# Third and fourth weight sums of a Strassen-like product started later in a pair, on GpSimd

## The reference

```
D_FF = 3 * D_MODEL; FFN_CONV = 3
h = rms_norm(x, g_ffn_pre)
up = h @ w_up                                  # (1024 x 1024) @ (1024 x 6144)
gate_h = causal_dwconv(up[..., :D_FF], ffn_conv_w, ffn_conv_b)
hid = gelu(gate_h) * up[..., D_FF:]
x = x + rms_norm(hid @ w_down, g_ffn_post)
```

## Time and profile before

| | us |
|---|---|
| median of 3 runs (lowest, highest) | 3272.5 (3272.47, 3274.01) |
| the profiled execution's own time | 3272.96 |
| its span in the trace | 3271.2 |
| PE busy | 3088.3 (94%) |
| DVE busy | 2314.0 (71%) |
| ACT busy | 1473.5 (45%) |
| POOL busy | 981.6 (30%) |

### The profile page before, as it was taken

One profiled execution on the slowest core, in us unless ns is written; L12 is line 12 of the kernel. 1 busy time (PEld: TensorE's weight loads), 2 busy tenths in 40 slices (PEclk: granted clock), 3 DMA queues, 4 the chain that ended last, 5 costly groups with the idle time before them and its releaser, 6 DMA issues.

```text
span 3271.2 us, 44920 instructions
## 1 busy us (share of the span) xinstructions
PE 3088.3 (94%) x14885; PEld 2455.6 (75%) x14885; DVE 2314.0 (71%) x2995; ACT 1473.5 (45%) x2003; POOL 981.6 (30%) x511
## 2 busy tenths in 40 slices
PE   6999998888998799999969999999989999999998
PEld 5668776566786688888857888888767777778867
DVE  7788967886545899999966775633588888811266
ACT  4345433667222788888841366201443343300142
POOL 2224342000341011111104433345234444434432
PEclk8999999999998899999989999999999999999999
DMA  7223221340242999999972222134133333454312
GB/s 263 71 63 93 65 65 52 110 120 30 81 160 85 378 382 379 380 382 382 352 267 60 64 83 87 41 120 145 64 91 104 114 103 108 155 206 148 115 33 71
DMA packets 365271, 496.54 MB, mean 152 GB/s; under 512 B 34478, under 2 KB 237148, under 8 KB 365156
## 3 DMA queue, kind: packets, MB, share of 16 engines
q1 hardware_dynamic: 350356, 460.39, 41.0%
q10 hardware_dynamic: 5440, 17.86, 1.7%
q0 software_dynamic: 9360, 16.80, 1.4%
HBM read 422.57 MB, written 83.92 MB: 155 GB/s over the span
## 4 chain that ended last, share of the span: by engine, by line
PE 43%; DVE 13%; issue 4%; SPq 3%; DMA 2%; ACT 2%; DVEq 0%; POOL 0%; ACTq 0%; POOLq 0%
PE acc L450 9%; PE acc L451 9%; PE acc L452 9%; PE acc L2049 3%; PE acc L2051 3%; PE acc L2050 3%; DVE TT L3064 3%; PE acc L2068 1%; PE acc L2070 1%; PE acc L2069 1%; DVE UWL L2817 1%; SPq L1952 1%; DVE uu L3070 1%; DVE TT L3073 1%; DMA mraw<-in_exp_w 1%
## 5 line engine op out<-in xcount | busy, mean ns | idle before, releaser
L421 POOL TENSOR_TENSOR whi<-wraw,one 128x1024 fp32r<-128x1024 f32 (+1 forms) x153 | 289.9, 1895 | 1312.2 <-PE acc L452 1014.4
L450 PE MATMUL acc<-Ah,whi 128*128 128x512 f32 (+1 forms) x1568 | 620.3, 396 | 4.6 <-POOL wlo L423 3.2
L452 PE MATMUL acc<-Ah,wlo 128*128 128x512 f32 (+1 forms) x1568 | 611.0, 390 | 0.0
L451 PE MATMUL acc<-Al,whi 128*128 128x512 f32 (+1 forms) x1568 | 611.0, 390 | 0.0
L423 POOL TENSOR_TENSOR wlo<-wraw,whi 128x1024 fp32r<-128x1024 f32 (+1 forms) x153 | 381.5, 2493 | 12.0
L450 PEld LDWEIGHTS acc<-Ah,whi 128*128 128x128 f32 (+1 forms) x1568 | 294.2, 188 | 81.5 <-issue 18.9
L451 PEld LDWEIGHTS acc<-Al,whi 128*128 128x128 f32 (+1 forms) x1568 | 294.4, 188 | 63.6 <-issue 3.1
L452 PEld LDWEIGHTS acc<-Ah,wlo 128*128 128x128 f32 (+1 forms) x1568 | 294.2, 188 | 62.6
L2162 DVE TENSOR_TENSOR mlo<-mraw,mhi 128x1024 fp32r<-128x1024 f32 x256 | 306.9, 1222 | 37.5 <-ACT mhi L2106 23.8
L2106 ACT ACTIVATE mhi<-mraw 128x1024 fp32r<-128x1024 f32 x256 | 267.8, 1063 | 74.5 <-PE acc L2051 51.6
L2049 PE MATMUL acc<-mhi,XTh 128*128 128x512 f32 x512 | 203.8, 398 | 3.6 <-DVE XTl L2157 3.3
(11 more groups left out here) (726 smaller groups left out, 6651.0 us busy)
## 6 DMA issues: line engine op xcount, KB each, us to landing
mraw<-in_exp_w SPq DMA_DIRECT2D x512, 256.0 KB
mraw<-in_exp_w SPq DMA_DIRECT2D x128, 512.0 KB, 12.1
wraw<-in_w_in SPq DMA_DIRECT2D x72, 512.0 KB, 3.8
TT<-in_ada_w SPq DMA_DIRECT2D x32, 512.0 KB, 3.8
TT<-gates SPq DMA_DIRECT2D x32, 512.0 KB, 4.6
wraw<-in_w_up SPq DMA_DIRECT2D x24, 512.0 KB, 4.7
hidTh<-hidh SPq DMA_DIRECT2D x24, 512.0 KB, 2.6
hidTl<-TT SPq DMA_DIRECT2D x24, 512.0 KB, 3.6
```

The source lines that it names most:

```text
L421: ch(pool.tensor_tensor(hi[:, r, 0:k, 0:m], wraw[:, r, 0:k, 0:m], one[:, 0:1].unsqueeze(2).broadcast_to([P, k, m]), ALU.mult))
L450: pe.matmul(o, hi[:, hr, j, 0:m], ih[:, k0 + j, cols], start=(j == 0), stop=False)
L451: pe.matmul(o, hi[:, hr, j, 0:m], il[:, k0 + j, cols], start=False, stop=False)
L452: last = pe.matmul(o, lo[:, hr, j, 0:m], ih[:, k0 + j, cols], start=False, stop=(j == k - 1))
```

## The change

POOL is made to wait twice more. Before the third sum for pair `m` it waits for `u_mid` to reach 3`m`-2, which is the end of result sum e of pair `m`-1. Before the fourth it waits for 3`m`-1, the end of f of pair `m`-1. Nothing else is altered; the first and second sums, the conditions that the sums had already, and L2650 stay where they are. The sums for pair 1, which are written apart, are not touched.

```diff
         def sums(m, odd, land):
             pool.wait_ge(S(f"uraw{odd}"), land)
             first_sums(pool, m, odd)
+            pool.wait_ge(S("u_mid"), 3 * m - 2)
             third_sum(pool, m, odd, US4)
+            pool.wait_ge(S("u_mid"), 3 * m - 1)
             fourth_sum(pool, m, odd)
             last_low(pool, m, odd)
```

## The result

The changed kernel takes 3285.46 us (median of 7 runs, 3282.22 to 3287.28) against 3274.01 for the kernel before, timed again beside it (7 runs, 3272.47 to 3276.75). The ratio is 1.0034, with a 95% interval of 1.0022 to 1.0046: about 11 us slower, where 11 us faster was forecast. The profiled execution took 3284.55 us with a span of 3282.8.

The account below looks back on a forecast made before the run. DVE was taken to set the pace, with PE waiting for its f. The terms gave -0.70 us even and -0.44 odd, -0.57 a pair; over 19 pairs 10.8 us, so 3261.5 us median (3262 profiled), range 3257 to 3283.

Parts of the forecast that it names:

- exclusive turn: A POOL sum and a DVE instruction with two SBUF inputs do not run together: one blocks the other.
- Terms 1 and 2: Second convolution step: -0.78 us even, 0 odd; low 0 undisturbed at 0.69: -0.77 even, -0.79 odd.
- term 3: Low 1: odd pair falls to 0.68 us, -0.50; waiting for ACT ahead of it adds +0.25 in both pairs.
- Term 5: POOL's fourth sum follows the third and blocks low 2, +0.60 us in each pair.
- its other case: POOL gets in between low 1 and L3073; f itself then releases the fourth sum, costing low 2 +0.57 us.
- step 4: POOL's third sum, released by e's end, gets its turn behind L3073, runs beside f and costs 0.
- A DVE stream without a gap keeps the turn: At boundaries between back-to-back DVE instructions, a waiting POOL sum is passed over until the stream ends; third sum costs 0.
- A: Rival: POOL's third sum gets in between low 1 and L3073; +0.49 us a pair, 3282 us, chance 0.31.
- G: Theory from A, tested in the runs: a waiting POOL sum gets in at the boundary between gapless DVE instructions.

Follow-up runs that it names:

- e1: The changed kernel with the third sum released by ACT's second weight copy in place of the end of e; 3287.81 us, ratio 1.0044 to before.
- e2: The changed kernel without the fourth sum's added wait, so only the third sum's wait is added; 3295.85 us, ratio 1.0067 to before.
- e6: As e1, with one more DVE subtraction of low 1's inputs and size ahead of low 1; 3299.82 us in one run.
- e8: The changed kernel with the third sum released once L3073 was handed over, in place of the end of e; 3284.20 us, ratio 1.0028 to before.
- e9: As e6, with the extra subtraction's result also in low 1's type (fp32r); 3298.74 us in one run.
- e5: The changed kernel with the third sum released by the end of L3073 and the fourth by the end of 22; 3258.91 us, ratio 0.9958 to before.
- e4: The changed kernel with the third sum released by the end of L3073 in place of the end of e; 3269.03 us, ratio 0.9988 to before.

## Why the prediction was wrong

*Right.* DVE's pace sets the stage's, and what it saves or loses reaches the end: 1.19 us more in two pairs over some 20 pairs is 12 us, 11 were measured. The exclusive turn held, and nothing behind POOL's waits was late. Terms 1 and 2 came as worked out: the convolution step -0.80 (forecast -0.78), low 0 -0.77 and -0.79. Of term 3 the 0.17 wait for ACT ahead of low 1 came; its 0.68 for low 1 did not, for the reason below. Term 5 came at +0.63 (forecast +0.60), but by another path: the fourth sum was released by f and not by the third, which the forecast had only in its other case, at +0.57.

*Wrong: step 4, the third sum at a price of 0.* It failed at two points.

1. *When POOL asks.* I had the sum ask 0.15 behind its start, so that low 1 would be ahead of it. In the changed kernel the sum started 0.16 behind e's end, low 1 0.17 behind it, and the sum took the turn. In e1, where it starts 0.13 behind low 1, low 1 has it. In all 20 pairs of the loop the order of these two starts goes with who is first, even by 0.01. My 0.15 was the difference between a sum alone (1.30) and a sum behind a release of the turn (1.15). But low 1 has nearly the same difference, 0.69 alone and 0.55 behind a release: if it is time before an instruction claims the turn, both engines have it, and I counted it for POOL alone.
2. *Who goes on at a boundary.* "A DVE stream without a gap keeps the turn" is what the low, positive or zero price hung on. It was drawn from the earlier trace rows, two places with other instructions, against the earlier trace rows, one place with the very two at hand. e1, e2, e6, e8 and e9 all show POOL getting in. The nearest row was the right one. The trace of before also had a place that the forecast didn't look at, a stream of four like DVE instructions. Its timelines of DVE, taken in four short windows, and of POOL:

```profile
844.44 1.23 DVE L1548 TENSOR_TENSOR Al<-OD,Ah 128x1024 fp32r<-128x1024 f32 x1 [12.56 <-ACT Ah L1539]
845.58 1.22 DVE L1548 TENSOR_TENSOR Al<-OD,Ah 128x1024 fp32r<-128x1024 f32 x1
846.72 2.06 DVE L1548 TENSOR_TENSOR Al<-OD,Ah 128x1024 fp32r<-128x1024 f32 x1
848.70 2.30 DVE L1548 TENSOR_TENSOR Al<-OD,Ah 128x1024 fp32r<-128x1024 f32 x1
...
845.58 2.12 POOL L421 TENSOR_TENSOR whi<-wraw,one 128x512 fp32r<-128x512 f32 x1 [109.12 <-PE acc L452]
847.78 2.15 POOL L423 TENSOR_TENSOR wlo<-wraw,whi 128x512 fp32r<-128x512 f32 x1
```

POOL stood waiting twice in this stream and got in both times: its two instructions end at 847.70 and 849.93, and the third and fourth of DVE end some 1.08 behind them.

Either point alone gives a price of about 1.1. With the measured price of low 1 (+1.14 even, +0.63 odd, where it had been 1.18 before) the sum closes. Even: -0.80 - 0.77 + 0.25 + 1.14 + 0.63 = +0.45, measured 20.62 - 20.16 = +0.46. Odd: -0.79 + 0.25 + 0.63 + 0.63 = +0.72, measured 20.19 - 19.46 = +0.73.

*The rivals.* A had the mechanism (the third sum stops DVE for 1.1 us and f is late) and nearly the price (+0.49 a pair, measured +0.60), but the wrong victim: low 1 and not L3073, whose 1.21 did not move. The Trainium skill, "SBUF — State Buffer", section "Who interferes with whom", has issue order decide who blocks, and as order of starts the traces of the stage agree, by 0.01 us in the changed kernel. They don't as order of handing over, which e8 shows. The earlier trace rows fit the order of starts no better: there POOL started before later DVE instructions and went behind them. The odds given to the forecast and to A were the wrong way round.

*Open.* Why POOL was passed over in the earlier trace rows isn't settled. Neither likeness of the instructions (e9) nor their being handed over before POOL was released (e8) brings it back. The stream of four above speaks against the length of the stream as the cause. There is one more such place in the trace of before, in pair 1; DVE's lines, then POOL's:

```profile
2413.91 0.68 DVE L2817 TENSOR_TENSOR UWL<-wraw,UWH 128x512 fp32r<-128x512 f32 x1
2414.51 0.68 DVE L2817 TENSOR_TENSOR UWL<-TT,UWH 128x512 fp32r<-128x512 f32 x1
...
2414.38 1.96 POOL L2650 TENSOR_TENSOR UWL<-wraw,UWH 128x512 fp32r<-128x512 f32 x1 [5.75 <-ACT UWH L2812]
```

POOL starts 0.13 ahead of low 5, is passed over, and ends at 2416.34, 1.15 behind low 5. The three places are the same in the traces of the changed kernel and of e1, e5, e6 and e8, so they are no accident of one execution. At all three the instructions of both engines stand outside the loops; where POOL got in, at least one of the two stands in a loop (in the earlier trace rows POOL's, in the last third sum of e1, from 2837.86, DVE's). No run parts this from the rest, so it is a pattern and not a cause shown. G holds at every place in this stage's loop, and not everywhere in the kernel.

## What to carry to other kernels

Before work of GpSimd is moved to "later", list for each place what VectorE runs there: in this loop a sum cost the part of its time by which it overran the stretch in which VectorE read no two operands from SBUF. The stretches here were behind a product and ahead of an instruction that waits for ScalarE, and between instructions that read PSUM; each is entered by a release of its own. For the first that is the end of the product. For the second the end of 22 served: the sum starts 0.44 us ahead of it, at a price of 0.29 (e5). The end of e leads into neither. Where two rows disagree on who yields, give most of the chance to the one with the same instructions, keep the other as the rival, and search the whole trace for further places before either becomes a rule.

## What the runs showed of the hardware

- A POOL 128x512 sum started 0.01 us ahead of a VectorE instruction with two SBUF inputs goes first, runs its 1.28 us undisturbed, and the 128x512 one ends 0.55 behind it (the changed kernel). A 128x1024 one that waits for a sum ends 1.08 behind it (e1, e2, e8).
- A waiting POOL sum gets in between two VectorE instructions whose records overlap by 0.08 us, even when the second had been handed over 0.4 us before it started (e8). So it was in e1, e2, e6, e8, e9 and twice from 845.58 to 848.78 before; at three other places of before (60.31, 2395.51, 2414.38) POOL was passed over.
- VectorE instructions with one input in PSUM keep their 0.68 or 0.69 beside a running POOL sum (L3118 in e5, L3109 in e4).
